# Two transformer layers on one core: constant matmuls at the start, transfers taken off GpSimd

## What is computed

```python
def first_block(x, ...):
    h = rmsnorm(x, attn_norm_g); z = h @ w_in              # 2048 x 5200
    u_pool, q, k, v, q_idx, k_idx, w_idx = split(z)
    q, k = rmsnorm(q, q_norm_g), rmsnorm(k, k_norm_g)
    y = concat(pool_mixer(u_pool), dsa_attention(q, k, v, q_idx, k_idx, w_idx))
    x = x + y @ w_out
    return x + conv_ffn(rmsnorm(x, ffn_norm_g), w_up, conv_w, conv_b, w_down)

def second_block(x, ...):
    proj = rmsnorm(x, attn_norm) @ w_in                    # q_a, k_a, v_a, c_q, c_kv, k_r, gates
    y_a = moba_attention(rope(q_a), rope(k_a), v_a)
    y_b = mla_attention(norm(c_q) @ w_uq, norm(c_kv) @ w_ukv, rope(k_r))
    g = sigmoid(gates)
    x = x + (g_a * (y_a @ w_branch_a) + g_b * (y_b @ w_branch_b)) @ w_out
    hn = rmsnorm(x, ffn_norm)
    x = x + (silu(hn @ w_gate) * (hn @ w_up)) @ w_down
    return rmsnorm(x, final_norm)
```

## Time and profile before

| | before |
|---|---|
| median of three runs | 2383.08 us |
| the profiled execution | 2383.49 us |
| its span, first to last instruction | 2381.6 us |
| mean granted TensorE clock | 0.998 |
| DVE busy | 58% |
| POOL busy | 5% |
| HBM read | 448.12 MB, 189 GB/s over the span |

### The profile page before, as it was taken

How to read it: one execution, slowest core, us unless ns; L and a number is a source line. 1 busy time by engine, 2 the same in 40 slices (tenths; PEclk the granted TensorE clock), 3 DMA queues, 4 the chain that set the end, 5 groups by cost and what they waited for, 6 DMA issues and landing times.

```text
span 2381.6 us, 29812 instructions
## 1 busy us (share of the span) xinstructions
PE 2365.1 (99%) x10624; PEld 1958.6 (82%) x10624; DVE 1390.7 (58%) x1574; ACT 1194.4 (50%) x1489; POOL 128.8 (5%) x228
## 2 busy tenths in 40 slices
PE   9999999999999999999999999999999999999997
PEld 7788888888888888888888888888888888888886
DVE  6785465776766765555554554766555555555543
ACT  6455455666666544445455544555444444444442
POOL 0100010000000000002130000122000000000000
PEclk9999999999999999999999999999999999999999
DMA  8775467788787766666776556666777777776554
GB/s 303 194 206 173 146 224 211 217 225 216 205 226 219 207 215 202 203 203 195 202 193 198 162 164 186 210 219 215 211 201 200 210 202 210 202 200 221 194 194 136
DMA packets 443082, 483.52 MB, mean 203 GB/s; under 512 B 208000, under 2 KB 225808, under 8 KB 442864
## 3 DMA queue, kind: packets, MB, share of 16 engines
q1 hardware_dynamic: 437712, 474.83, 67.7%
q0 software_dynamic: 4704, 6.44, 1.0%
q10 hardware_dynamic: 576, 1.05, 0.1%
HBM read 448.12 MB, written 2.10 MB: 189 GB/s over the span
## 4 chain that ended last, share of the span: by engine, by line
PE 97%; SPq 1%; issue 0%; DMA 0%; ACT 0%; DVE 0%; POOLq 0%; POOL 0%; DVEq 0%; ACTq 0%
PE acc L727 31%; PE acc L729 31%; PE acc L728 31%; SPq L504 1%; PE pair_banks L898 1%; PE bank L718 0%; PE pair_banks L929 0%; PE acc L753 0%; PE acc L757 0%; PE acc L760 0%; DMA w_raw<-in_w_in 0%; PE pair_banks L959 0%; PE pair_banks L870 0%; PE pair_banks L930 0%; SPq L373 0%
## 5 line engine op out<-in xcount | busy, mean ns | idle before, releaser
L1430 DVE TENSOR_TENSOR w_lo<-w_raw,w_hi 128x1024 fp32r<-128x1024 f32 (+1 forms) x842 | 1024.7, 1220 | 928.3 <-ACT w_hi L1068 926.7
L1068 ACT ACTIVATE w_hi<-w_raw 128x1024 fp32r<-128x1024 f32 (+1 forms) x842 | 886.2, 1055 | 1051.4 <-PE acc L729 1003.3
L727 PE MATMUL acc<-w_hi,xT 128*128 128x512 f32 (+1 forms) x2208 | 862.7, 391 | 0.0
L729 PE MATMUL acc<-w_hi,xT 128*128 128x512 f32 (+1 forms) x2208 | 857.1, 388 | 0.0
L728 PE MATMUL acc<-w_lo,xT 128*128 128x512 f32 (+1 forms) x2208 | 856.6, 388 | 0.0
L727 PEld LDWEIGHTS acc<-w_hi,xT 128*128 128x128 f32 x2208 | 414.6, 188 | 86.9 <-issue 2.3
L729 PEld LDWEIGHTS acc<-w_hi,xT 128*128 128x128 f32 x2208 | 414.5, 188 | 85.7
L728 PEld LDWEIGHTS acc<-w_lo,xT 128*128 128x128 f32 x2208 | 414.7, 188 | 83.5
L727 PE MATMUL acc<-w_hi,f_hi 128*128 128x512 f32 x688 | 267.6, 389 | 0.0
L728 PE MATMUL acc<-w_lo,f_hi 128*128 128x512 f32 x688 | 267.6, 389 | 0.0
L729 PE MATMUL acc<-w_hi,f_lo 128*128 128x512 f32 x688 | 267.6, 389 | 0.0
(11 more groups left out here) (220 smaller groups left out, 1308.4 us busy)
## 6 DMA issues: line engine op xcount, KB each, us to landing
w_raw<-in_w_up SPq DMA_DIRECT2D x264, 512.0 KB, 4.2
w_raw<-in_w_in SPq DMA_DIRECT2D x198, 512.0 KB, 3.8
w_raw<-in_w_down SPq DMA_DIRECT2D x176, 512.0 KB, 4.6
w_raw<-in_w_gate SPq DMA_DIRECT2D x88, 512.0 KB, 3.6
w_raw<-in_w_out SPq DMA_DIRECT2D x64, 512.0 KB, 4.6
w_raw<-in_w_branch_a SPq DMA_DIRECT2D x16, 512.0 KB, 4.2
w_raw<-in_w_branch_b SPq DMA_DIRECT2D x16, 512.0 KB, 4.8
halves<-stage SPq DMA_DIRECT2D x208, 32.0 KB, 2.6
```

Of the source, the lines that this page charges most:

```text
L727: pe.matmul(o, l, w_hi[:, slot, k, 0:width], start=start, stop=False)
L729: last = pe.matmul(o, m, w_hi[:, slot, k, 0:width], start=False, stop=stop)
L1068: act.activation(in_slot(w_hi, slot, width), in_slot(w_raw, slot, width), ACT.Copy).then_inc(w_split_hi, 1)
L1430: dve.tensor_tensor(in_slot(w_lo, slot, width), in_slot(w_raw, slot, width), in_slot(w_hi, slot, width).bitcast(F32), ALU.subtract).then_i ...
```

## The change

1. PE: `warm(8)` and two more constant matmuls of 256 columns instead of `warm(6)`; and in chunks 0 and 1 one constant matmul of 256 columns ahead of the second and of the third wait of each half.
2. The moves of x and of the mix: for n < 3 all sixteen are issued by SP, four at each of the steps b to b+3, and the split stands at step b+7 instead of b+3. For n = 3 SP issues eight at step b as before, and ACT the other eight at step b. One semaphore for both.
3. The five constants are loaded by SP behind the loads of chunks 19 to 23, and `pool_w` by SP at a step of its own. POOL issues nothing.
4. The moves of units qn1, qr2 and qa1 stand 2, 4 and 4 steps later, and `copy_k` for ka units two steps later.

```diff
@@ plan
+        later = {("qn", 1): 2, ("qr", 2): 4, ("qa", 1): 4}.get((name, half), 0)
         for b in range(4):
-            put(n + lead + b, "move", u, g, b)
+            put(n + lead + later + b, "move", u, g, b)
         if name in ("k1", "ka"):
-            put(n + lead + 6, "copy_k", u, g)
+            put(n + lead + (6 if name == "k1" else 8), "copy_k", u, g)
...
         if gain is not None:
-            put(b, "move_x", 0)
-            put(b, "move_x", 1)
-            put(b + 3, "split_x", n, gain)
+            for part in range(4) if n < 3 else (None,):
+                put(b + (part or 0), "move_x", n + 4 * quarters, part)
+            put(b + (7 if n < 3 else 3), "split_x", n, gain)
...
+    put(b + 19, "load_pool")
...
-        put(b, "move_mix", 0); put(b, "move_mix", 1); put(b + 3, "split_mix", n)
+        for part in range(4) if n < 3 else (None,):
+            put(b + (part or 0), "move_mix", n, part)
+        put(b + (7 if n < 3 else 3), "split_mix", n)
@@ shared
+        def move_blocks_of(queue, part, first_half, to, from_, done):
+            for k in range(4) if part is not None else range(8):
+                b, a_ = (part, k) if part is not None else (k // 2, k % 2 + (0 if first_half else 2))
+                move_block(queue, to, from_, b, a_).then_inc(done, 16)
+        def move_x(queue, n, part, first_half):
+            queue.wait_ge(x_blocks, NT * (n + 1))
+            move_blocks_of(queue, part, first_half, flat_stage[1], flat_stage[0], x_moved)
@@ sync
                 if not chunk.per:
+                    if 20 <= chunk.now < 25:
+                        load_constant(chunk.now - 20)
                     for step_, *args in at.get(chunk.now - RING - LEAD - 1, []):
-                        if step_ == "move_x" and args[0] == 0:
-                            move_x(sp, x_moves, 0)
+                        if step_ == "move_x":
+                            move_x(sp, *args, True)
...
+                        elif step_ == "load_pool":
+                            sp.wait_ge(rel_full, 6)
+                            sp.dma_start(pool_w[:], ...).then_inc(pool_loaded, 16)
@@ tensor
                     for k, t in both:
                         pe.matmul(... xT_hi ... w_hi ...)
+                    if c < 2:
+                        warm(1, S)
                     pe.wait_ge(x_lo_ready, kts)
...
+                    if c < 2:
+                        warm(1, S)
                     pe.wait_ge(*((w_half_lo, c + 1) if ks == (0,) else (w_split_lo, c + 1)))
...
-            def warm(count):
+            def warm(count, width=CW):
+                moving = y_lo[:, 0:2].rearrange("p k s -> p (k s)")[:, 0:width]
                 for _ in range(count):
-                    pe.matmul(acc[1][0][:], y_lo[:, 0, 0:P], ..., start=True, stop=True)
+                    pe.matmul(acc[1][0][:, 0:width], y_lo[:, 0, 0:P], moving, start=True, stop=True)
             pe.wait_ge(warm_set, 1)
-            warm(6)
+            warm(8)
+            warm(2, S)
@@ scalar
+            def on_move_x(n, part):
+                if part is None:
+                    move_x(act, n, part, False)
+            def on_move_mix(n, part):
+                if part is None:
+                    move_mix(act, n, part, False)
             def on_split_x(n, gain):
                 n_x[0] += 1
-                for half in range(2):
-                    act.wait_ge(x_moved[half], 16 * 8 * n_x[0])
+                act.wait_ge(x_moved, 256 * n_x[0])
```

More of the change, by code:

```diff
@@ L104, in attend, with residual @@
         put(a + 7, "split_y", which, pair)
-    def residual(n, g, b, gain):
+    def residual(n, g, b, gain, quarters=None):
         put(b, "res", g, n)
@@ L146, in plan @@
         b = group("w_out", CW * n, CW, [0, 1, 4, 5, 6, 7, 2, 3] if n == 0 else whole, "y")
-        residual(n, len(groups) - 1, b, G_FFN1)
+        residual(n, len(groups) - 1, b, G_FFN1, 0)
     up1 = b
@@ L356, in two_layer_kernel @@
         unit_blocks, unit_moved, k_copied = sem("unit_blocks"), [sem(f"unit_moved{k}") for k in range(4)], sem("k_copied")
-        mix_blocks, mix_moved = sem("mix_blocks"), [sem("mix_moved_sp"), sem("mix_moved_pool")]
+        mix_blocks, mix_moved = sem("mix_blocks"), sem("mix_moved")
         mix_high, mix_low = sem("mix_high"), sem("mix_low")
         x_blocks, x_high, x_low = sem("x_blocks"), sem("x_high"), sem("x_low")
-        x_moved = [sem("x_moved_sp"), sem("x_moved_pool")]
+        x_moved = sem("x_moved")
         dve_step, pool_step, normalised = sem("dve_step"), sem("pool_step"), sem("normalised")
@@ L373, in move_block, with move_mix @@
             return queue.dma_start(dst, src)
[L375 to L389, removed]
+        def move_blocks_of(queue, part, first_half, to, from_, done):
[5 more added lines that the diff above has]
+            move_blocks_of(queue, part, first_half, flat_stage[1], flat_stage[0], x_moved)
+        def move_mix(queue, n, part, first_half):
+            queue.wait_ge(mix_blocks, n + 1)
+            move_blocks_of(queue, part, first_half, flat_half, flat_stage[1], mix_moved)
         def turned(unit, q):
@@ L453, in _ @@
         def _(sp):
-            chunk, products, x_moves, mix_moves = Count(), Count(), [0, 0], [0, 0]
+            chunk, products = Count(), Count()
             def load_x(n):
@@ L482, in load, with load_constant @@
                 if not chunk.per:
+                    if 20 <= chunk.now < 25:
+                        load_constant(chunk.now - 20)
                     for step_, *args in at.get(chunk.now - RING - LEAD - 1, []):
-                        if step_ == "move_x" and args[0] == 0:
-                            move_x(sp, x_moves, 0)
-                        elif step_ == "move_mix" and args[0] == 0:
-                            move_mix(sp, mix_moves, 0)
+                        if step_ == "move_x":
+                            move_x(sp, *args, True)
+                        elif step_ == "move_mix":
+                            move_mix(sp, *args, True)
+                        elif step_ == "load_pool":
+                            sp.wait_ge(rel_full, 6)
+                            sp.dma_start(pool_w[:], a["pool_w"].rearrange("w (k p) d -> p w k d", p=P)).then_inc(pool_loaded, 16)
                         elif step_ == "move":
                             move_unit(*args)
+            def load_constant(k):
+                if k == 0:
+                    sp.dma_start(cols[:, CONV_COL:], a["columns"][:, CONV_COL:]).then_inc(taps_loaded, 16)
+                elif k == 1:
+                    sp.dma_start(causal[:], a["c_causal"]).then_inc(const_loaded, 16)
+                elif k == 2:
+                    sp.dma_start(pool_m[:], a["c_pool"]).then_inc(const_loaded, 16)
+                elif k == 3:
+                    sp.dma_start(cos[:, 0, :], a["c_freq"]).then_inc(const_loaded, 16)
+                else:
+                    sp.dma_start(pos_i[:], a["positions_2"][0, :].rearrange("(t p) -> p t", p=P),
+                                 allow_slow_non_contiguous=True).then_inc(const_loaded, 16)
             def move_unit(u, g, b):
@@ L594, in _ @@
         def _(pool):
[L597 to L607, removed]
+            n_rstd, n_heads, n_roped, n_lat, steps = [0], [0], [0], [0], [0]
             def step(ins):
@@ L683, in on_rope @@
                 pool.sem_inc(roped, 1)
-            mine = {"headsq": on_heads, "rstd": on_rstd, "rstd0": on_rstd, "lat_rstd": on_lat, "rope": on_rope,
-                    "move_x": on_move_x, "move_mix": on_move_mix}
+            mine = {"headsq": on_heads, "rstd": on_rstd, "rstd0": on_rstd, "lat_rstd": on_lat, "rope": on_rope}
             for n in range(n_end + 8):
                 for step_, *args in at.get(n, []):
-                    if step_ == "isc" and args[0] == 5:
-                        pool.wait_ge(rel_full, 6)
-                        pool.dma_start(pool_w[:], a["pool_w"].rearrange("w (k p) d -> p w k d", p=P)).then_inc(pool_loaded, 16)
                     if step_ in mine:
@@ L1218, in on_split_mix @@
             def on_split_mix(n):
-                for half in range(2):
-                    act.wait_ge(mix_moved[half], 16 * 8 * (n + 1))
+                act.wait_ge(mix_moved, 256 * (n + 1))
                 for q in range(4):
@@ L1266, in _ @@
                     "copy_p": on_copy_p, "copy_d": on_copy_d, "copy_kr": on_copy_kr, "copy_kn": on_copy_kn,
-                    "split_y": on_split_y, "split_x": on_split_x, "split_pool": on_split_pool,
+                    "split_y": on_split_y, "split_x": on_split_x, "move_x": on_move_x, "move_mix": on_move_mix, "split_pool": on_split_pool,
                     "split_lat": on_split_lat, "split_mix": on_split_mix, "square": on_square,
```

13 lines of the change are left out of this document (2 added, 11 removed).

## The result

| | before | after |
|---|---|---|
| median (lowest to highest) | 2382.61 us (2382.31 to 2383.52) | 2391.27 us (2389.97 to 2393.43) |
| ratio after/before, 95% interval | | 1.0037 [1.0026, 1.0048] |
| profiled execution: time, span | 2383.49, 2381.6 us | 2390.44, 2388.7 us |

The changed kernel is slower by 0.37%, 8.7 us. The forecast was 2391.3 us. That the two numbers agree is partly luck: the trace shows two terms that the forecast did not have, -5.3 and +2.7 us, and one that it had and that did not come. This part shows where each microsecond went.

The account below looks back on a forecast made before the run. PE bounds the kernel, busy 2365.1 of 2381.6 us. Start -0.5, middle -2.1, w_out/w_up 1.7, w_down/w_in_2 1.6, mix 5.8, w_out_2/w_gate_2 1.7 give +8.2 us: median 2391.3 us, range 2384 to 2398.

Parts of the forecast that it names:

- Part 1: Start: added constant products raise the clock earlier, so chunk 2 starts at 12.5 us; -0.5 us, bounds -1.4 and +0.9.
- Part 2: Middle, near 1200 us: later unit moves and key copy remove three PE pauses; -2.1 us, bounds -2.1 and 0.
- Part 3: Third quarter's split at its deadline: PE waits 1.5 us before w_up and w_gate_2, 3.6 at the mix, none before w_in_2.
- Part 4: ACT's eight last-quarter moves delay w_hi: 0.2 us before w_up and w_gate_2, 1.6 before w_in_2, 2.2 at the mix.
- the deciding point: How long ACT takes to issue one move: 0.64 us like SP's in the forecast, 0.44 like its own loads otherwise.
- rival 1: Not slower: ACT issues a move in 0.44 us and the mix's loads land in time; +1.9 us, 2385.0 us; chance 0.25.
- The last quarter at the mix: At the mix, ACT's eight issues make w_lo ready at 1580.1 where PE wants it at 1577.9; +2.2 us.
- each wait adds: Delays at one place were summed; at the mix 3.6 us for the split and 2.2 for ACT's issues made 5.8.
- POOL's own rows end nowhere near the path: End of the kernel: taking POOL's transfers away was costed at nothing, 0 us.
- rival 2: ACT and SP share a descriptor path, 1.28 us per move, 5.1 us more at four places; 2411.7 us; chance 0.06.
- rival 4: Faster: neither split nor issue delays PE, middle and start pay in full; -3.5 us, 2379.6 us; chance 0.01.
- rival 3: Start: clock rises as late as before and PE pays the constants; +1.4 us on the forecast, 2392.7 us; chance 0.07.

Follow-up runs that it names:

- experiment 1: Kernel before with only the new start (extra constant products ahead of the leading product and in chunks 0 and 1): 2384.11 us, ratio 1.0004.
- experiment 9: Kernel of experiment 8 with the third quarter of w_out and w_out_2 moved like the fourth, split at b+4: 2377.28 us, 0.9977 against the kernel before.
- experiment 10: Kernel of experiment 9 with the old start (six constant products, none in chunks 0 and 1): 2376.60 us, 0.9974 against the kernel before.
- experiment 2: Kernel before with only the later moves of qn, qr, qa and the later latent-key copy: 2380.64 us, ratio 0.9990.
- experiment 6: Changed kernel with the third quarter's split one step earlier (b+6) at x and mix: 2395.30 us; run again unchanged, 2393.88 us.
- experiment 7: Changed kernel with the mix as before (SP eight moves at b, POOL the other eight, split at b+3): 2383.40 us, 1.0000 against the kernel before.
- experiment 5: Changed kernel with twenty constant products of 512 columns in the pause before w_out_2's first chunk: 2392.08 us, 1.0036 against the kernel before.
- experiment 3: Changed kernel with the one load of pool_w issued by POOL again: 2391.43 us, 1.0036 against the kernel before.
- experiment 4: Changed kernel with ACT's eight last-quarter moves one step later at x, two at the mix: 2386.34 us, 1.0013 against the kernel before.
- experiment 8: Changed kernel, ACT's x moves at b+1, third x split at b+6, mix in whole halves with ACT two steps later: 2377.91 us, 0.9979 against the kernel before.

## Why the prediction was right, and where it was not

**Part 1, the start (-0.5; 0.7 in the profiles).** The count of matmuls was right: the product started at 5.47 us, forecast 5.48, and chunk 2 at 12.40, forecast 12.5. The moment of the clock's rise, which I counted on from one trace, is none of the kernel's. It was up at 4.5, 6.3, 7.4 and 10.2 us in executions with one start or the other, and the medians of experiments 1, 9 and 10 show no gain. The step that failed is taking the moment of one execution for the kernel's. The Trainium skill (TensorE: Matmul & The Clock Gate, "Part 1: The HAM clock gate") says that one and the same kernel starts with a different number of slow matmuls from run to run; the traces agree, with the old start's 10.2 and 6.6 us.

**Part 2, the middle (-2.1; -2.5).** Right in sign, place and nearly in size, alone too (experiment 2). That SP would be 4 us late cost nothing.

**Part 3, the late split.** 1.5 us each at 353.85 and 1662.28: the idle rows say 1.38 plus the 0.16 of a drawn matmul. Experiment 6 removes the first. At the mix the mechanism is right, with SP's issues to 0.04 us; the size was off (3.6 against 5.6) by two terms. The lateness that each quarter hands to the next was 1.5 to 1.6 us and not 0.8, so the third quarter's blocks were 1.5 us later than assumed, and a load landed in 5.1 us and not 4.6. 1.5 and 0.5 make up the 2.0. The rows show where the lateness came from. In the first quarter SP's second four moves took 3.15 us instead of 2.51, so the load of chunk b+11 left 12.85 us behind the blocks instead of 12.15. In the second it left in time but landed in 4.7 us, not 4.2, and ACT began its w_hi another 0.3 us later, held by the split that waited for its moves (0.69 us). The landing of a load in this stretch, 3.7 to 6.2 us, isn't the kernel's median of the earlier trace rows; that the moves beside it are the reason is not shown. Experiment 7 shows that all 8.4 us of the mix come from this part of the change.

**Part 4, ACT's issues.** The rows settle the deciding point between forecast and rival 1: eight issues took 5.43 us at 357 and 5.44 at 1576, 0.68 each, not 0.44 and not 1.28. Before w_in_2 they took 6.09 us (5.16 assumed, beside SP's slow first one, 5.76 for its eight), and DVE had turned the blocks at 1077.55 where before's pace, +1.50, gives the same. So w_lo of chunk 382 came 1.1 us later than the forecast had it: 2.7 us of waiting instead of 1.6. The 0.2 each before w_up and w_gate_2 came as 0.38 (0.22 idle) and 0.4. The Trainium skill's sentence (DMA: Bandwidth & Descriptors, "Issuing engines are not separate DMA queues") that the sequencer's time to start a transfer is "usually small relative to the DMA itself" does not hold here: a move of 32 KB takes 0.68 us of ACT and lands in 2.7 us, a quarter of it, and eight of them hold ACT for 5.4 us.

**The last quarter at the mix (+2.2; 0) and the clock (0; +2.7).** The trace of the changed kernel has the second and not the first. The row of DVE says how near they are:

```profile
1582.52 3.50 DVE L1440 TENSOR_TENSOR w_lo<-w_raw,w_hi 128x1024 fp32r<-128x1024 f32 x3 [6.67 <-ACT w_hi L1072]
```

The first of these three, w_lo of chunk 552, was done at 1583.74, and PE came to it at 1584.58. Without the 2.75 us of the low clock PE would have come at 1581.83 and waited 1.9 us (an estimate from these numbers), close to the 2.2 of the forecast. So the step "each wait adds" failed, and by luck: the clock's loss covered the wait, and only 0.8 us of it came on top. Nor does one simply replace the other. In the two profiles of experiment 6, where the first pause was shorter, both were paid in part, 1.7 us of slow clock and then 1.9 or 2.3 us of waiting, and in experiment 5 the wait brought a fall of the clock of its own.

**The end (0; -5.3).** The term I missed altogether, and larger than any but the mix. "POOL's own rows end nowhere near the path" was wrong: POOL's last row is a DRAIN that ends 5.6 us behind the last landing (2381.39 and 2375.83). With 0, 1, 32 and 134 transfers issued by POOL it took 0.646, 0.753, 3.287 and 11.127 us:

```profile
q0 software_dynamic: 4704, 6.44, 1.0%
```

```profile
q0 software_dynamic: 1024, 1.05, 0.2%
```

```profile
q0 software_dynamic: 272, 1.05, 0.1%
```

(POOL's queue in before, experiment 7 and experiment 3: packets, MB, share.) 272 packets cost 0.107 us and 1024 cost 2.64, while 1, 32 and 134 transfers cost 0.107, 0.083 and 0.078 us each: it goes by transfers, not by packets or bytes. It lies in parallel with the landing of the last stores, 5.6 us from its start, so some 62 of them would be free (an estimate: (5.6-0.65)/0.08); the 72 others would cost 5.8 us, and 5.3 were seen. Without this term the same change would have been slower by 14 us.

**Sum.** -0.7+2.2+2.8-2.5+5.6+2.7+0+2.2-5.3 = 7.0, against 7.1 between the spans. The forecast's terms gave 8.2. In the medians it is 8.7; the profiled execution of after lies 0.8 under its median, and by the profiles of experiments 4 to 7 what varies from one execution to the next is behind which pause the clock falls (3.3 us between the two of experiment 6) and how late the loads at the mix are (0.1 to 1.2 us lost before chunk 547). Rival 1 (2385.0), rival 2 (2411.7) and rival 4 are refuted by the 0.68 us of an issue and by the pauses; rival 3, for this execution, by the start's rows (12.40, not 14.0).

What stays open: what decides whether the clock falls behind a pause of 1.9 to 2.7 us (the rows show both, at the same place), whether the start's constants are worth anything at all, and why over_y landed 1.5 us later in experiment 1, and why the loads at the mix land when they do.

## What to carry to other kernels

Read the trace to its last row, barrier included, before saying that an engine is off the path. When transfers are moved from one queue to another, price them by issue time on the engine that gets them (here 0.64 us on SP and 0.68 on ACT, with everything behind them held up), and place them behind the work that the next product needs, not ahead of it: one step later took away a pause of 2.8 us. Two delays at one place don't add, and taking away one may show the other, so an edit that "must" save 1.5 us is worth its own run.

## What the runs showed of the hardware

- POOL's DRAIN at the end takes 0.65 us and about 0.08 us more for each transfer that POOL has issued in the whole kernel (11.13 us for 134), long after all of them have landed.
- The granted clock fell to the low level behind pauses of 5.4, 2.85, 2.65 and 1.88 us, and stayed up behind pauses of 2.55 and 1.90 us at the places of two of these. The chunk behind a fall took 4.0 to 5.3 us instead of 2.72. With constant products in the 5.4-us pause it stayed at 1.00 until the next pause.
- At the start of the kernel the clock's rise differed by some 3 us between executions that had the same instructions until then (6.6 and 10.2 us with the old start, 4.5 and 7.4 with the new).
- A move of 32 KB costs its issuing engine 0.68 us on ACT, at three places within 0.01, but eight took 6.09 us at 1077.58; in the other profiles they took 6.07 to 7.05 us at that same place, and in experiments 8 and 9 6.7 to 7.0 us at 335 and 1502 us. Why there, no run here shows.
